# Out-projection blocks in the last head's round of a gated recurrent layer, and one wait fewer in the other rounds

## The reference

```
q, f, i, g = split(h @ w_in, 4)
q = silu(q); forget = lb + (1 - lb) * sigmoid(f); k = 1 - forget; b = cumsum(log(forget)) in the chunk
o_intra = causal((q * exp(b - b_mid)) @ (k * exp(b_mid - b)).T) @ i
S_next  = exp(b_last) * S + (k * exp(b_last - b)).T @ i        # over the 8 chunks
o = o_intra + (q * exp(b)) @ S
o = rmsnorm(o) * gain * silu(g)                                # per head
m = o @ w_out                                                  # 1024 x 1024
x = x + rmsnorm(m)
```

## Time and profile before

| | |
|---|---|
| Median of three executions | 2423.66 us (2418.24 to 2430.54) |
| The profiled execution | 2418.41 us, its span 2416.5 us |
| Busy in the span | PE 2295.2 us (95%), VectorE 1299.5 (54%), ScalarE 957.6 (40%), GpSimd 432.0 (18%) |
| Mean granted clock of PE | 0.976 of full |
| DMA | 203.15 MB, 84 GB/s |

### The profile page before, as it was taken

How to read it: one execution, slowest core, us unless ns; L and a number is a source line. 1 busy time by engine, 2 the same in 40 slices (tenths; PEclk the granted TensorE clock), 3 DMA queues, 4 the chain that set the end, 5 groups by cost and what they waited for, 6 DMA issues and landing times.

```text
span 2416.5 us, 31380 instructions
## 1 busy us (share of the span) xinstructions
PE 2295.2 (95%) x11126; PEld 1866.4 (77%) x11126; DVE 1299.5 (54%) x1587; ACT 957.6 (40%) x1321; POOL 432.0 (18%) x331
## 2 busy tenths in 40 slices
PE   8999998999899999999999998589999999999997
PEld 7888886788778888878888876477778777888885
DVE  5454337666355454355454358967776635554433
ACT  5223334555443323333223336254554533422332
POOL 2121102111121121012121011126321102121100
PEclk9999998999899999999999999899999999999999
DMA  5332332222113333323332322122121122333231
GB/s 165 97 97 83 92 104 67 79 69 69 61 61 105 104 91 86 96 75 112 96 98 79 96 94 64 53 62 62 54 87 62 53 81 67 105 95 96 84 96 64
DMA packets 68587, 203.15 MB, mean 84 GB/s; under 512 B 8320, under 2 KB 12544, under 8 KB 68512
## 3 DMA queue, kind: packets, MB, share of 16 engines
q1 hardware_dynamic: 68512, 202.13, 27.6%
HBM read 199.94 MB, written 2.16 MB: 84 GB/s over the span
## 4 chain that ended last, share of the span: by engine, by line
PE 89%; DVE 7%; ACT 2%; issue 2%; DMA 0%; SPq 0%; DVEq 0%; ACTq 0%
PE bank L1631 73%; PE bank L1817 7%; DVE up L1144 1%; PE bank L1978 1%; DVE attn L1226 1%; PE bank L1957 1%; DVE w_lo L939 1%; DVE gate L1144 1%; PE bank L1778 0%; PE bank L1964 0%; DVE gd_o L1207 0%; DVE sq L1204 0%; PE bank L1969 0%; PE bank L1972 0%; PE bank L1775 0%
## 5 line engine op out<-in xcount | busy, mean ns | idle before, releaser
L939 DVE TENSOR_TENSOR w_lo<-raw,w_hi 128x1024 fp32r<-128x1024 f32 x405 | 587.1, 1467 | 482.2 <-ACT w_hi L519 482.1
L1631 PE MATMUL bank<-h_hi,w_hi 128*128 128x512 f32 x1760 | 703.1, 400 | 45.3 <-DVE h_lo L943 31.4
L1631 PE MATMUL bank<-h_hi,w_lo 128*128 128x512 f32 x1760 | 692.7, 394 | 0.0
L1631 PE MATMUL bank<-h_lo,w_hi 128*128 128x512 f32 x1696 | 666.6, 393 | 0.0
L519 ACT ACTIVATE w_hi<-raw 128x1024 fp32r<-128x1024 f32 x405 | 426.6, 1055 | 553.3 <-PE bank L1631 534.3
L1631 PEld LDWEIGHTS bank<-h_hi,w_hi 128*128 128x128 f32 x1760 | 335.3, 191 | 125.3 <-issue 33.2
L1631 PEld LDWEIGHTS bank<-h_hi,w_lo 128*128 128x128 f32 x1760 | 334.7, 190 | 71.7
L1631 PEld LDWEIGHTS bank<-h_lo,w_hi 128*128 128x128 f32 x1696 | 323.1, 190 | 69.1 <-issue 3.1
L1498 POOL TENSOR_TENSOR y<-y,up 128x512 f32<-128x512 f32 x88 | 173.9, 1977 | 745.9 <-DVE up L982 671.1
L1631 PE MATMUL bank<-act_hi,w_hi 128*128 128x512 f32 x704 | 277.4, 394 | 0.0
L1631 PE MATMUL bank<-act_hi,w_lo 128*128 128x512 f32 x704 | 276.0, 392 | 0.0
(11 more groups left out here) (266 smaller groups left out, 2312.8 us busy)
## 6 DMA issues: line engine op xcount, KB each, us to landing
raw<-in_ffn_in SPq DMA_DIRECT2D x172, 512.0 KB, 3.6
raw<-in_gd_in SPq DMA_DIRECT2D x49, 512.0 KB, 3.6
raw<-in_ffn_out SPq DMA_DIRECT2D x64, 384.0 KB, 3.1
raw<-in_ffn_out SPq DMA_DIRECT2D x64, 320.0 KB, 2.9
raw<-in_hg_in SPq DMA_DIRECT2D x32, 512.0 KB, 3.5
raw<-in_gd_out SPq DMA_DIRECT2D x16, 512.0 KB, 3.7
raw<-in_hg_out SPq DMA_DIRECT2D x8, 512.0 KB, 3.5
g_bc<-g_rows SPq DMA_DIRECT2D x8, 512.0 KB, 5.5
```

What stands on the lines that cost most here:

```text
L939: nc.vector.tensor_tensor(w_lo[:, r, :], raw[:, r, :], w_hi[:, r, :].bitcast(f32), ALU.subtract).then_inc(lo_split, 1)
L1631: ins = nc.tensor.matmul(dst, w, moving[ml][:, k, :], start=first and n == 0 and (wl, ml) == (0, 0), stop=last and n == len(ks) - 1 and wl ...
```

## The change

In the last round `piece` now calls `out_block`. It issues the first seven blocks of tile 0 into bank 0 and then those of tile 1 into bank 1, one block per place: 1 ahead of the v transposes, 1 ahead of the scores, 2 ahead of the state products, 4 ahead of the outputs, 1 ahead of the sum, 5 behind it. The first waits for `o_ready` of seven heads and for the drain of bank 0, the first of tile 1 for the drain of bank 1. `out_proj` then has one block left, that of the last head, in each of the two tiles. The k_end transposes wait for `g_scaled` in round 1 only, where g was in bank 3.

```diff
--- before.py
+++ after.py
@@ -24,6 +24,7 @@
 UNIT = KD * P
 RING = 4
 HEADS = 8
+EARLY_HEADS = 7
 CH = 64
 NCH = TOK // CH
 NT = TOK // P
@@ -1672,7 +1673,7 @@
                         pe.wait_ge(act_ready, n0 + max(k + 1, KF - 2))
                 out_proj(s, (act_hi, act_lo), ready)
 
-            def out_proj(s, moving, ready):
+            def out_proj(s, moving, ready, begun=0):
 
                 cuts = CUTS[kinds[s]]
                 n_u = len(cuts) - 1
@@ -1688,7 +1689,10 @@
                             k = t * n_u + q
                             u = (v0 + k, 4 * i) if not isinstance(i, int) else (v0 + k + 4 * i, 0)
                             pe.wait_ge(lo_split, count(u) + 1 + SKEW)
-                            if peeled and t == 0:
+                            if peeled and t < begun:
+                                ready(EARLY_HEADS)
+                                ins = blocks(bank[t][:], u, EARLY_HEADS, moving, [EARLY_HEADS], False, True)
+                            elif peeled and t == 0:
                                 for k in range(cuts[q], cuts[q + 1]):
                                     ready(k)
                                     ins = blocks(bank[t % 2][:], u, k - cuts[q], moving, [k], k == 0, k == cuts[-1] - 1)
@@ -1712,11 +1716,29 @@
                     free = (f_scaled if first else q_scaled, i_scaled if first else g_scaled, f_scaled, i_scaled)
                     at = [0]
 
+                    def out_block():
+
+                        c, k = at[0] // EARLY_HEADS, at[0] % EARLY_HEADS
+                        at[0] += 1
+                        if c == 2:
+                            return
+                        if at[0] == 1:
+                            pe.wait_ge(o_ready, EARLY_HEADS)
+                            pe.wait_ge(q_scaled, HEADS)
+                        if k == 0:
+                            pe.wait_ge(lo_split, u0 + IN_UNITS["hg"] + c + 1 + SKEW)
+                        if c == 1 and k == 0:
+                            pe.wait_ge(g_scaled, HEADS)
+                        blocks(bank[c][:], (u0 + IN_UNITS["hg"] + c, 0), k, (o_hi, o_lo), [k], k == 0, False)
+
                     def piece():
 
+                        if not gemm:
+                            out_block()
+                            return
                         t, p = at[0] // 4, at[0] % 4
                         at[0] += 1
-                        if not gemm or t == 4:
+                        if t == 4:
                             return
                         u = (u0 + t, 4 * j)
                         if p == 0:
@@ -1727,7 +1749,7 @@
                             ins.then_inc(unit_used, 1)
 
                     piece()
-                    if first:
+                    if first and gemm:
 
                         for _ in range(4):
                             piece()
@@ -1749,7 +1771,8 @@
                                      q_cen[:, t * P:(t + 1) * P], start=True, stop=True)
                         ins.then_inc(scores_made, 1)
                         pe.wait_ge(k_end_ready, j)
-                        pe.wait_ge(g_scaled, j)
+                        if first and j == 1:
+                            pe.wait_ge(g_scaled, 1)
                         wait(pe, o_logged, j - 1)
                         for t in range(NT):
                             ins = nc.tensor.transpose(bank[3][:, t * P:(t + 1) * P], k_end[:, t * P:(t + 1) * P], ident[:])
@@ -1778,7 +1801,7 @@
                                     ins = MM(bank[2][:, n * CH:(n + 1) * CH], state[:, n - 1, :],
                                              q_int[:, n * CH:(n + 1) * CH], start=False, stop=n % 2 == 1)
                         ins.then_inc(o_made, 1)
-                    for _ in range(3):
+                    for _ in range(3 if gemm else 1):
                         piece()
                     if chain:
                         pe.wait_ge(o_squared, j)
@@ -1793,7 +1816,7 @@
 
                 def ready(k):
                     pe.wait_ge(o_ready, k + 1)
-                out_proj(s, (o_hi, o_lo), ready)
+                out_proj(s, (o_hi, o_lo), ready, begun=2)
 
             def deltanet(s):
                 MM = nc.tensor.matmul
```

## The result

The changed kernel takes 2404.86 us in the median of eight runs (2401.29 to 2414.34), the kernel before 2418.3 in the median of eight (2416.76 to 2430.54): a ratio of 0.9948, 95% interval 0.9935 to 0.9961, clear of 1 (the quotient of the two medians, 0.9944, lies inside it). That is 13.4 us between the medians, 12.6 between the spans of the two profiled executions (2416.5 and 2403.9). Lines behind the edit are numbered higher: L1740 is L1762 now, L1748 L1770, L1755 L1778, L1765 L1788, L1775 L1798, L1785 L1808; lines of `blocks`, DVE and ACT are one higher.

What follows compares the result with a forecast made beforehand. TensorE (PE) was taken as the bound, holding 89% of what ended last. 5.6 + 9.0 - 1.3 = 13.3 us took the profiled 2418.41 to 2405.1; from the median 2423.66 the forecast was 2410.4, range 2401 to 2418.5.

Steps and rivals of the forecast that it cites:

- Part 1: Heads 2 to 7: without the k_end transposes' wait on g_scaled their idle time closes, 5.6 us.
- slacks that start from a matmul of the same round: Heads 2 to 7: 0.84 us at q_in and 1.20 at the scores, said not to shrink when rounds get shorter.
- void part 1: Rival, heads 2 to 7: another release replaces g_scaled and the wait's removal gives nothing; 2416.0 us, chance 0.14.
- Part 2: Last round: 14 out-projection blocks moved into it let tile 2 start 9.0 us earlier, before the clock's fall is taken off.
- blocks 1 and 2: Last round, ahead of the scores: said to cost 0.1 us at most, counted as nothing.
- The step that the clock would stay full: Last round: PE nearly full from 620.2 to 624.9, so full clock taken; L1765 lasts 1.16 us, not 2.04.
- The half-clock round: Rival: half clock through the whole last round; 6.5 us gained with part 1, 2417.2 us, chance 0.10.
- the lasting low clock at tile 2: Rival, out-projection: the clock's fall lasts over three tiles (72 matmuls, 15.1 us); 2432.3 us, chance 0.04.
- The fall: Start of tile 2: the new 2.3 us gap may drop the clock; cost taken as 1.3 us, bounds 0 and 2.6.
- the row of 444.30: Earlier trace: after a gap of 2.25 us the matmul lasted 0.47, full clock; evidence for no fall.
- the forecast case: Whole kernel: both parts gain and the clock falls at the new gap; median 2410.4 us, chance 0.42.
- the rival without a fall: Rival, start of tile 2: the clock stays full at the new gap; sum 14.6 us, 2409.1 us, chance 0.18.

Runs made afterwards that it cites:

- experiment 1: Kernel before with only the k_end transposes' wait on g_scaled removed after round 1, no block moved: 2411.76 us, ratio 0.9972.
- experiment 3: Changed kernel with no block moved: nine discarded blocks up to the sum, five places behind it empty, out-projection whole: median 2411.32 us over 12 runs.
- experiment 8: Changed kernel with all 14 blocks behind the sum, none in the gaps ahead of it: 2411.5 us.
- experiment 4: Changed kernel with three more, discarded blocks in the 2.35 us gap ahead of the last head's block: 1.4 us faster between medians, 1.0 in the layer.
- experiment 2: Changed kernel with the wait on g_scaled put back in every round, so the moved blocks alone: 2410.30 us, ratio 0.9975.
- experiment 6: Changed kernel with the out-projection's tiles through four banks, each waiting for the copy four tiles before, not two: one run only, 12.1 us in the layer.

## Why the prediction was right, and where it was off

**Part 1.** Forecast 5.6, measured 5.7 in the changed kernel and the same 0.85 a round in experiment 1. The reading that the gate's drain alone released the transposes was right, and no other wait came up: slacks that start from a matmul of the same round did not shrink. The rival of a void part 1 is out.

**Part 2.** Forecast 9.0 less 1.3, measured 8.0. Each link stands within 0.1 of the forecast up to the last head's block (table above), and blocks 1 and 2, counted at nothing, held the scores up by 0.1. The step that the clock would stay full because PE is nearly full carried half of it, as experiments 3 and 8 show: useless blocks in the gaps give 4.8, of which 4.0 are the clock and 0.8 the wait's removal, and useful ones behind the sum give nothing beyond that removal. The half-clock round is out, and so is the lasting low clock at tile 2: it was full again after three matmuls of that tile.

**The fall.** Taken at 1.3, measured 1.0 by experiment 4. The prediction set the row of 444.30 (no fall) against the last round (a fall); but the gap at 444.30 itself goes either way: a gap of this length drops the clock in some executions and not in others (last section). That the forecast case and not its rival was met is to that extent luck. Experiment 2's execution went as the rival without a fall, and tile 2 then started 2.12 after the last head's block, 2.15 forecast. The rule of the Trainium skill (TensorE: Matmul & The Clock Gate, "What's actually happening"), by which a fall needs a whole idle stretch, would have put the changed kernel on the rival's side; in the traced execution PE had worked until 631.98 and was at work again at 634.33, and the clock fell, so the trace doesn't agree with it.

**Sum and median.** Forecast 13.3, measured 13.4 between medians and 12.6 between spans. What was off is the last step, "It is itself 5.3 below the median of the runs shown, so I forecast 2410.4 for the median": the profiled execution was the typical one, and the median of three the odd one. Eight runs have their median at 2418.3. The sum made against the profiled execution, 2405.1, met the 2404.86. That 13.3 meets 13.4 so closely is partly luck: the layer alone won 13.7, 0.4 more than forecast, and what came behind it took 1.3 back in the profiled execution.

**Not foreseen.** The 1.3 us given back behind the layer, in the feed-forward step and in the second layer's mixer. In the traces the work there is the same and the stretches at half clock lie otherwise: behind the gap of 4.69 us at the feed-forward step twelve matmuls are slow in the changed kernel (677.15 to 682.41), ten were before. That the shift in time is what moved them is argued, not shown.

## What to carry to other kernels

An idle gap in a serial chain costs twice where it drops TensorE's clock: the idle time itself, and the links behind it, which then run at half clock. Filling it with work that is needed later wins back both. Where the work is put decides: with nine of the 14 blocks ahead of the sum the last round gained 8.0 us, with all 14 behind it 0.6, which is no more than the wait's removal gives. Ask of every wait on a shared engine whether it guards a buffer in this iteration or only in a peeled one. And when a forecast is made against one profiled execution, its distance to a median of three runs is no correction to add.

## What the runs showed of the hardware

The gap of 2.25 us in round 2 (released by q_in's drain) stands in all ten profiled executions. The clock fell behind it in three (experiments 1, 2 and 6, 0.86 over 440 to 452) and stayed full in seven. Behind the gap of about 2.36 us in the last round it fell in two (the changed kernel, experiment 6) and not in one (experiment 2). So the same gap in the same code has either outcome. What a fall costs depends on what stands behind it: in round 2 it cost 1.6 us in experiments 1 and 6, but 0.2 in experiment 2, which keeps the wait on g_scaled, where PE would have been idle anyway.

In the second layer's mixer PE waits some 25 us for VectorE (25.1 in the changed kernel) and comes back at half clock. How long it then stays so differs between executions, though the code is the same and PE is busy. Changed kernel, and then experiment 4, the same stretch:

```profile
1526.00:1544.00 18.00, 16.95 (x182) 13.88 (x177) 17.54 (x27) 8.29 (x17) 4.89 (x4) 1.00 0.26 83
```

```profile
1526.00:1544.00 18.00, 17.22 (x126) 14.26 (x125) 12.68 (x18) 6.55 (x13) 3.33 (x3) 0.64 0.28 88
```

In the changed kernel PE is back at 1522.3 and the clock is full some 3 us later; in experiment 4 PE is back at 1519.7 and works at half clock for some 19 us. The offset of experiment 4 to the kernel before goes from -15.3 at the split of 1496.92 to -8.9 at 1558.20: 6.4 us lost, so its span (2407.4) is longer than that of the changed kernel though its gated layer is 1 us shorter. This is the size of the spread of the runs, 2401.3 to 2414.3 for the changed kernel, where the granted clock is 0.979 to 0.982 in the six faster runs and 0.976 and 0.975 in the two that took over 2412. Only one execution of each kernel has a trace, and those two don't, so whether it is this stretch in them is open.
